# Issue places of the modulation loads, and the spread of the modulation steps over TensorE's turns

## The reference

```
mod   = (silu(c)     @ w_ada + b_ada)      # 6 parts of 2048: sh1, sc1, g1, sh2, sc2, g2
mod_c =  silu(c_ctx) @ w_ada + b_ada
hc = rmsnorm(ctx) * (1 + csc1) + csh1      # parts 0 and 1
hl = rmsnorm(x)   * (1 + sc1)  + sh1       # parts 0 and 1
hl @ w_in -> hyena (3072), xbc (1536), z (1024);   hc @ w_in -> xbc only
x = x + g1 * mixer(hl);  hl2 = rmsnorm(x) * (1 + sc2) + sh2;  x = x + g2 * mlp(hl2)   # parts 2 to 5
```

## Time and profile before

| | |
|---|---|
| median of 3 runs | 4540.35 us |
| profiled execution, its own time | 4543.01 us |
| its span, from first to last instruction | 4541.2 us |
| mean granted TensorE clock | 0.94 |
| PE busy | 3987.4 us (88%) |
| DVE busy | 2912.3 us (64%) |
| ACT busy | 2153.3 us (47%) |
| DMA | 704.5 MB, mean 155 GB/s |
| modulation loads (ada_ring) | 192 of 512 KB, median 5.5 us from issue to landing |
| mix_in weight loads (ring from in_w_mix) | 88 of 512 KB, median 6.9 us |

### The profile page before, as it was taken

One profiled execution on the slowest core, in us unless ns is written; L12 is line 12 of the kernel. 1 busy time (PEld: TensorE's weight loads), 2 busy tenths in 40 slices (PEclk: granted clock), 3 DMA queues, 4 the chain that ended last, 5 costly groups with the idle time before them and its releaser, 6 DMA issues. The chain is left out here.

```text
span 4541.2 us, 69428 instructions
## 1 busy us (share of the span) xinstructions
PE 3987.4 (88%) x21628; PEld 3260.5 (72%) x21628; DVE 2912.3 (64%) x5320; ACT 2153.3 (47%) x3715; POOL 149.7 (3%) x64
## 2 busy tenths in 40 slices
PE   6699968578999998969788998449999999999998
PEld 0467735477888887746577877347888888888887
DVE  0544435587776667599676557796666666666667
ACT  0433311244555554522344434168777776555554
POOL 3000000000000000033101000000000000000000
PEclk9899979888999999989898999679999999999999
DMA  9686610044666664600154535104666666666665
GB/s 333 234 320 233 241 31 0 1 148 149 189 189 190 190 187 141 186 2 1 37 176 148 170 117 166 61 0 131 189 188 188 190 189 186 189 185 191 189 189 162
DMA packets 199677, 704.50 MB, mean 155 GB/s; under 512 B 29687, under 2 KB 29720, under 8 KB 198808
## 3 DMA queue, kind: packets, MB, share of 16 engines
q1 hardware_dynamic: 199096, 698.43, 48.6%
q0 software_dynamic: 480, 4.81, 0.3%
HBM read 701.06 MB, written 2.10 MB: 155 GB/s over the span
## 5 line engine op out<-in xcount | busy, mean ns | idle before, releaser
L212 DVE TENSOR_TENSOR weights_lo<-ring,weights_hi 128x512 fp32r<-128x512 f32 x2240 | 1510.7, 690 | 1005.0 <-ACT weights_hi L205 990.5
L205 ACT ACTIVATE weights_hi<-ring 128x512 fp32r<-128x512 f32 x2240 | 1389.9, 631 | 1351.5 <-PE ps L749 1186.6
L749 PE MATMUL ps<-expert_parts,weights_hi 128*128 128x512 f32 x4224 | 1456.0, 393 | 10.8 <-DVE expert_parts L709 7.4
L749 PE MATMUL ps<-expert_parts,weights_lo 128*128 128x256 f32 x4224 | 1140.5, 280 | 0.0
L749 PEld LDWEIGHTS ps<-expert_parts,weights_hi 128*128 128x128 f32 x4224 | 777.3, 188 | 170.6 <-issue 8.4
L749 PEld LDWEIGHTS ps<-expert_parts,weights_lo 128*128 128x128 f32 x4224 | 796.1, 188 | 21.9
L749 PE MATMUL ps<-mlp_parts,weights_hi 128*128 128x512 f32 x1024 | 353.6, 394 | 16.0 <-PEq L519 16.0
L749 PE MATMUL ps<-hidden,weights_hi 128*128 128x512 f32 x1024 | 351.2, 392 | 0.0
L749 PE MATMUL ps<-att_parts,weights_hi 128*128 128x512 f32 x768 | 271.1, 400 | 29.6 <-DVE att_parts L709 28.0
L749 PE MATMUL ps<-mlp_parts,weights_lo 128*128 128x256 f32 x1024 | 276.9, 281 | 0.0
L749 PE MATMUL ps<-h_parts,weights_hi 128*128 128x512 f32 x704 | 266.0, 405 | 11.8 <-DVE weights_lo L212 11.8
(11 more groups left out here) (440 smaller groups left out, 5126.3 us busy)
## 6 DMA issues: line engine op xcount, KB each, us to landing
ring<-in_w_mlp SPq DMA_DIRECT2D x256, 512.0 KB, 3.6
ring<-in_w_u SPq DMA_DIRECT2D x256, 512.0 KB, 4.2
ring<-in_w_v_tab SPq DMA_DIRECT2D x256, 512.0 KB, 4.2
ada_ring<-in_w_ada SPq DMA_DIRECT2D x192, 512.0 KB, 5.5
ring<-in_w_mix SPq DMA_DIRECT2D x88, 512.0 KB, 6.9
ring<-in_w_out SPq DMA_DIRECT2D x64, 512.0 KB, 3.6
ring<-in_w_in SPq DMA_DIRECT2D x48, 512.0 KB, 3.9
ring<-in_w_q SPq DMA_DIRECT2D x32, 512.0 KB, 3.6
```

The source lines that it names most:

```text
L205: act.activation(core.hi[:, g % SLOTS], core.ring[:, slot, at:at + QUARTER], ACT.Copy).then_inc(core.rounded, 1)
L212: dve.tensor_tensor(core.lo[:, g % SLOTS], core.ring[:, slot, at:at + QUARTER], core.hi[:, g % SLOTS].bitcast(F32), ALU.subtract).then_inc ...
L749: mm = pe.matmul(out, part[:, g % SLOTS, k, :], moving, start=at == 0 and part is core.hi, stop=last and part is core.hi)
```

## The change

Three things change, all for the stage mix_in.

1. Time is counted in turns: a tile of a layer with one right-hand side is one turn, a tile with two right-hand sides is two (24 + 24 + 8 = 56, of which 4 are spare). done(t) is (t+1)*64//52, and 0 for negative t. In the XBC layer a cluster now stands behind the second and behind the fourth quarter.
2. SyncE's modulation loads of turn t go up to number 4 + 2*done(t-2). In XBC each half tile is a turn and issues its own; in HY and Z the loads stand behind the first half tile's weight load of a turn (slot 2t), none behind the second's.
3. ScalarE's modulation copy stands in the take of the tile that holds turn over+1, and the turn on TensorE in the cluster of turn over+2, where over is the turn in which the part's steps end.

```diff
--- before.py
+++ after.py
@@ -404,22 +404,22 @@
 class ModulationBeside:
 
 
-    def __init__(self, mod, parts, tiles, spare):
-        self.mod, self.parts, self.tiles = mod, parts, tiles - spare
+    def __init__(self, mod, parts, turns, spare):
+        self.mod, self.parts, self.turns = mod, parts, turns - spare
         self.first = parts[0] * 2 * KD
         self.steps = len(parts) * KD
 
     def done(self, t):
-        return min(self.steps, (t + 1) * self.steps // self.tiles)
+        return max(0, min(self.steps, (t + 1) * self.steps // self.turns))
 
     def first_loads(self, sp):
         for n in range(self.mod.SLOTS):
             self.mod.load(sp, self.first + n)
 
-    def loads(self, sp, slot):
-
-        upto = lambda n: min(2 * self.steps, self.mod.SLOTS + 2 * self.steps * n // (2 * self.tiles))
-        for n in range(upto(slot), upto(slot + 1)):
+    def loads(self, sp, t, fresh):
+
+        free = lambda n: min(2 * self.steps, self.mod.SLOTS + 2 * self.done(n - 2))
+        for n in range(free(t - 1) if fresh else free(t), free(t)):
             self.mod.load(sp, self.first + n)
 
     def tensor(self, pe, t):
@@ -431,12 +431,12 @@
                 self.mod.turn(pe, part)
 
     def over(self, j):
-        return next(t for t in range(2 * self.tiles) if self.done(t) >= (j + 1) * KD)
-
-    def scalar(self, act, t):
+        return next(t for t in range(2 * self.turns) if self.done(t) >= (j + 1) * KD)
+
+    def scalar(self, act, turns):
 
         for j, part in enumerate(self.parts):
-            if self.over(j) + 1 == t:
+            if self.over(j) + 1 in turns:
                 self.mod.copy(act, part)
 
     def vector(self, dve):
@@ -579,8 +579,8 @@
     begun, begin_next = core.begun, begin_next and next_w is not None
     before = 0
     for layer in layers:
-        layer.before = before
-        before += layer.tiles
+        layer.before, layer.turns = before, len(layer.rhs)
+        before += layer.tiles * layer.turns
 
         layer.Q, layer.N, layer.M, layer.S, layer.A = core.quarters, core.tiles, core.moves, core.shapes, core.sources
         core.quarters += layer.tiles * layer.quarters
@@ -623,10 +623,10 @@
             if beside is not None:
                 beside.first_loads(sp)
             for layer, after in zip(layers, layers[1:] + [None]):
-                at = layer.before * layer.quarters // 2
                 stream(core, sp, layer.w, layer.tiles * layer.quarters // 2,
                        next_w if after is None else (after.w, after.first), layer.first, layer.Q,
-                       None if beside is None else lambda n: beside.loads(sp, at + n))
+                       None if beside is None else lambda n: beside.loads(
+                           sp, layer.before + (n if layer.turns == 2 else n // 2), layer.turns == 2 or n % 2 == 0))
             if loads:
                 sp.wait_ge(loaded, 16 * len(loads))
 
@@ -673,7 +673,8 @@
                         act.wait_ge(core.summed, i * layer.unroll + (layer.N + s + 3))
                         layer.shape(act, n, slots(layer, n, s)).then_inc(core.shaped, 1)
                     if beside is not None:
-                        beside.scalar(act, layer.before + n)
+                        at = layer.before + n * layer.turns
+                        beside.scalar(act, range(at, at + layer.turns))
                 return take
             run(act, make_hi, source_of, take_of)
 
@@ -760,8 +761,9 @@
                     pe.wait_ge(core.summed, i * layer.unroll + (layer.N + s + 1))
                     for q in range(layer.quarters):
                         products(pe, layer, i, s, q)
-                    if beside is not None:
-                        beside.tensor(pe, layer.before + i * layer.unroll + s)
+                        if beside is not None and (q + 1) * layer.turns % layer.quarters == 0:
+                            n = i * layer.unroll + s
+                            beside.tensor(pe, layer.before + n * layer.turns + (q + 1) * layer.turns // layer.quarters - 1)
 
             for layer in layers:
                 if beside is not None:
@@ -1409,7 +1411,7 @@
                     conv3_layer(core, "w_mix", XBC_TILES, [h_parts, ctx_parts], HY_TILES, [xbc, xbc_ctx],
                                 core.prm["ssd_conv_w"], core.prm["ssd_conv_b"], [GRID, T]),
                     Layer("w_mix", Z_TILES, [h_parts], shape=silu_z, first=2 * (HY_TILES + XBC_TILES)),
-                ], ("w_out", 0), beside=ModulationBeside(mod, (2, 3, 4, 5), HY_TILES + XBC_TILES + Z_TILES, 4))
+                ], ("w_out", 0), beside=ModulationBeside(mod, (2, 3, 4, 5), HY_TILES + 2 * XBC_TILES + Z_TILES, 4))
             dt_stage(core, wdt, h_parts, ctx_parts, ssd, xbc, xbc_ctx)
         with ExitStack() as hyena:
             sb2 = lambda name, shape: hyena.enter_context(nc.sbuf_tensor(name, shape, F32))
```

## The result

The changed kernel takes 4611.45 us (median of 4 runs, 4609.05 to 4612.1), the one before 4542.57 beside it: ratio 1.0149, 95% interval [1.0136, 1.0162], so 68.9 us more. Forecast were +58.9 us (4599 us, within 4560 to 4622). The profiled execution took 4609.05 us, 66.0 more than the one of before.

The account below looks back on a forecast made before the run. The prediction took TensorE, busy 88% of the span, as the bound; -25.6 + 1.6 + 53.4 + 1 + 2.7 + 25.8 = +58.9 us on the 4540.35 median gave 4599 us, range 4560 to 4622.

Parts of the forecast that it names:

- waits of before: First and third layers of mix_in: TensorE's old losses all go because bandwidth is no longer short, -25.6 us.
- more and other clusters: Mix_in: 12 clusters of two steps and 40 of one, instead of 24 and 16, +1.6 us.
- late loads, 12 places, with clock: One-sided layers of mix_in: clusters wait for late modulation loads, +53.4 us, and the clock drops behind them, +25.8.
- second layer, small waits: Second layer of mix_in: at most 0.3 us missing per cluster, +1 us for all, 0 to 3.
- copy at turn 27, with clock: End of XBC tile 1: TensorE's turn waits for ScalarE's late copy of mod_rows, +2.7 us, once.
- the clock: TensorE behind the twelve late-load waits: a lower granted clock, 6 * 1.5 + 6 * 2.8 = +25.8 us.
- C - 1.4: One-sided layers: modulation loads issue 1.4 us before C, the end of tile t-1 and start of its cluster.
- Rival A: Mix_in: waits come as forecast but the clock is hardly lost, +33 us, 4573; chance 0.22.
- the upper bound of 36: TensorE's clock loss in mix_in if every wait pays: 13 * 2.8 = 36 us.
- The rule of the Trainium skill: TensorE: an engine waiting for a DMA between bursts starts each at the low clock; every wait pays, 36 us.
- Rivals B and C: Mix_in: B, loads in time, 4519 us, chance 0.07; C, saving and late loads cancel, within 5 of 4541, chance 0.04.
- some 24 us faster: Mix_in loads: the old order of issue with the new spread would be the good half, some 24 us faster.

Follow-up runs that it names:

- e2: The kernel before with the new load rule alone, keeping the old spread of steps: 4726.06 us, ratio 1.0405 to the kernel before.
- e6: The changed kernel with modulation loads issued ahead of SyncE's wait for the split: 4537.24 us, ratio 0.9987 to the kernel before.
- e8: The changed kernel with unused matmuls on TensorE just before each of the 12 late steps: 4598.35 us, ratio 1.0116 to the kernel before.
- e11: The old spread of steps over output tiles, with the modulation loads placed as in e9: 4536.22 us, ratio 0.998 to the kernel before.
- e1: The changed kernel's new spread of steps with the old load rule, in proportion to time: 4534.85 us, ratio 0.9982 to the kernel before.
- e10: e9 with a part's turn three turns behind its last step instead of two: 4530.7 us, ratio 0.9972 to the kernel before.
- e9: The changed kernel, one-sided layers' loads in the other half tile, modulation loads ahead of SyncE's split wait: 4533.71 us, ratio 0.9978 to the kernel before.

## Why the prediction was right, step by step

In us, for the stage; "measured" from the windows above by the same working:

| term | forecast | measured |
|---|---|---|
| waits of before | -25.6 | -25.6 |
| more and other clusters | +1.6 | +4.1 |
| late loads, 12 places, with clock | +53.4 + 25.8 = 79.2 | 63.1 + 11.4 + 0.5 = 75.0 |
| second layer, small waits | +1 | +4.4 |
| copy at turn 27, with clock | +2.7 | +5.6 |
| sum | +58.9 | +63.5 |

The sum is nearer than its terms: the clock was 8.4 us too large, and the other terms together 13.0 too small (waits 4.2, clusters 2.5, second layer 3.4, copy 2.9). That they nearly cancel is luck. Of the 10.0 us between +58.9 and +68.9 in the medians 4.6 lie in the stage.

- **The mechanism** was as told: issue at C - 1.3 (C - 1.4), TensorE's waits 2.70 and 3.62 us (2.5 and 3.5), at the named turns and at no others. e2 and e6 show it from both sides: more such clusters, 184 us; the loads ahead of the wait, nothing.
- **Late loads, the wait part, a little too small.** The second modulation load landed 4.8 to 5.6 us behind C at eleven places and 6.6 at turn 17, not 4.9. Taking the end of each cluster as its last landing plus 1.0 us gives 57.6 us for the twelve, against 53.4.
- **Clock, too large.** The same working leaves 17.4 us (75.0 - 57.6), and e8 took 14.9 away; the forecast had 25.8. I had priced a wait of 3.5 us like the one of 2.78, with 2.8 us. In the trace the dip after a single step costs 0.9 us in the half step and 0.9 in the tile: much of the low stretch lies over the wait itself, where nothing is lost (granted clock 0.50 from 199.50 to 201.16, ahead of the step). Rival A (no clock loss, +33) is ruled out by e8, the upper bound of 36 by the table. The rule of the Trainium skill that the prediction names ("TensorE: Matmul & The Clock Gate", HAM oscillation) holds in its direction, but not for every wait: of the 12 tiles behind a late cluster 8 were slower by 0.8 to 1.0 us, one by 0.5, two by 0.1 to 0.2 and one (at 271.64, behind a wait of 2.69 us) not at all.
- **Clusters, a term missing.** A cluster inside an XBC tile breaks its stream of matmuls. The starts show it, half a tile after the change first, then a whole tile before it:

```profile
389.41 0.50 PE L750 MATMUL ps<-h_parts,weights_hi 128*128 128x512 f32 x1
...
395.16 0.64 PE L367 MATMUL ps<-ada_ring,silu_c 128*32 128x512 f32 x4
...
366.10 0.50 PE L749 MATMUL ps<-h_parts,weights_hi 128*128 128x512 f32 x1
...
377.39 1.07 PE L367 MATMUL ps<-ada_ring,silu_c 128*32 128x512 f32 x8
```

  Half a tile takes 5.75 us; a whole one took 11.29 before (and so the 154.38 us of the earlier trace rows less clusters and a turn, by 12). 12 * (11.50 - 11.29) = 2.5 us. The start of a cluster had been read as free.
- **Copy at turn 27.** The wait was 2.7 us as forecast. The turn behind it ran at the low clock, which makes 3.6 us in the cluster, and the next tile took 2.0 us more; I had bounded this clock loss and not taken it.
- **Second layer.** One cluster (turn 25) was 2.0 us longer for a load in front of which another took 1.0 us to issue; five others were 0.1 to 0.9 us longer.
- **Outside the stage** +2.5 us in the profiled execution, and the medians are 2.9 further apart than the two profiles. Not explained; the 3.4 us before the experts are in e11 too, which has nothing of this change.
- **Rivals B and C** had SyncE reach the loads earlier; it did not, at any tile.
- **Bandwidth.** "All 25.6 us go" holds nearly as far as the spread goes (e1 has 6.4 us of waits left). The "some 24 us faster" that the prediction gave for the old order of issue with the new spread is e1, and it was 8.8 us in the stage. And the best kernel, e10, gains 16.6 of them: 4.1 go into clusters, 4.9 into remaining waits.

## What to carry to other kernels

Ask of each load in a ring when its slot comes free, and where the queue reaches it; the lead is landing time against the distance from that place to the first use, and with a ring of two steps there is none to give away. A queue that stands waiting in front of a load is no loss as long as what is behind it has lead of its own: here 192, 197 and 284 us of SyncE's waiting in the stage went with the fast variants e10, e9 and e1, and 2 us with the slow one. When a wait is shown to be long, move what stands behind it ahead of it, before making the load wait for something later.

## What was not expected of the hardware

- Filling a wait of TensorE with matmuls that nobody uses kept the granted clock at 1.00 through all twelve waits and was worth 14.9 us of a 480 us stage (15.9 without the first tile).
- A break in a stream of products by a 128x32 cluster costs 0.2 us in the stream beside the cluster's own 0.99 us.
